# First pointwise stage of a convolution block: split weights, tap products on ScalarE, tap sums in PSUM

## The reference

```python
def conformer_conv(h, w_pw1, b_pw1, w_dw, b_dw, ln_g, ln_b, w_pw2, b_pw2):
    u = h @ w_pw1 + b_pw1                  # 2048 -> 4096: value and gate
    a, gate = jnp.split(u, 2, axis=-1)
    u = a * jax.nn.sigmoid(gate)
    u = depthwise_conv(u, w_dw, 31 taps, padding 15) + b_dw
    u = jax.nn.silu(layer_norm(u, ln_g, ln_b))
    return u @ w_pw2 + b_pw2
```

## Time and profile before

| | |
|---|---|
| time, median of 3 runs | 2646.93 us (2645.94 to 2649.62) |
| the profiled execution | 2647.79 us, of which its span of instructions 2645.9 us |
| PE busy | 2595.2 us, 98% of the span |
| DVE busy | 1874.5 us, 71% |
| ACT busy | 1232.9 us, 47% |
| POOL busy | 129.3 us, 5% |
| TensorE's mean granted clock | 0.99 of full speed |
| DMA | 560.60 MB, mean 212 GB/s |

### The profile page before, as it was taken

One profiled execution on the slowest core, in us unless ns is written; L12 is line 12 of the kernel. 1 busy time (PEld: TensorE's weight loads), 2 busy tenths in 40 slices (PEclk: granted clock), 3 DMA queues, 4 the chain that ended last, 5 costly groups with the idle time before them and its releaser, 6 DMA issues. The chain is left out here.

```text
span 2645.9 us, 40988 instructions
## 1 busy us (share of the span) xinstructions
PE 2595.2 (98%) x15425; PEld 2277.4 (86%) x15425; DVE 1874.5 (71%) x2655; ACT 1232.9 (47%) x1617; POOL 129.3 (5%) x203
## 2 busy tenths in 40 slices
PE   6999899999999999999999999999999999999998
PEld 4899898888888888888888888888888888888887
DVE  3468778887888888855666659999776644566554
ACT  3345544445645556544555541105554443444443
POOL 0021122001010000000000000000000000000000
PEclk8999999999999999999999999999999999999999
DMA  9998699768786877755666554554666655666554
GB/s 367 334 306 252 210 271 298 220 199 248 236 267 211 256 249 245 233 189 187 190 189 188 187 159 144 151 153 132 190 186 190 189 187 188 191 186 189 189 183 135
DMA packets 525076, 560.60 MB, mean 212 GB/s; under 512 B 20453, under 2 KB 487841, under 8 KB 524688
## 3 DMA queue, kind: packets, MB, share of 16 engines
q1 hardware_dynamic: 504448, 487.39, 58.1%
q0 software_dynamic: 20496, 71.38, 9.0%
...
...
## 5 line engine op out<-in xcount | busy, mean ns | idle before, releaser
L1126 DVE TENSOR_TENSOR wlo<-raw,whi 128x1024 fp32r<-128x1024 f32 x794 | 970.4, 1224 | 663.8 <-ACT whi L697 657.2
L697 ACT CAST whi<-raw 128x1024 fp32r<-128x1024 f32 x794 | 830.7, 1050 | 1037.1 <-PE ps L1944 896.5
L1942 PE MATMUL ps<-xhl,whi 128*128 128x512 f32 x3584 | 1130.6, 397 | 3.6 <-DVE xhl L1204 2.1
L1944 PEld LDWEIGHTS ps<-xhl,wlo 128*128 128x128 f32 x3584 | 674.3, 188 | 159.5
L1944 PE MATMUL ps<-xhl,wlo 128*128 128x256 f32 x3584 | 705.0, 278 | 0.0
L1942 PEld LDWEIGHTS ps<-xhl,whi 128*128 128x128 f32 x3584 | 547.0, 189 | 7.2 <-issue 5.1
L1942 PE MATMUL ps<-ghl,whi 128*128 128x512 f32 x1024 | 319.5, 393 | 0.0
L1944 PEld LDWEIGHTS ps<-ghl,wlo 128*128 128x128 f32 x1024 | 192.2, 188 | 44.5
L2304 PE MATMUL ps<-xg,raw 128*128 128x256 f32 x1024 | 221.5, 379 | 0.0
L1942 PE MATMUL ps<-fhl,whi 128*128 128x512 f32 x704 | 219.3, 392 | 0.0
L2304 PEld LDWEIGHTS ps<-xg,raw 128*128 128x128 f32 x1024 | 194.5, 190 | 26.4
...
## 6 DMA issues: line engine op xcount, KB each, us to landing
...
raw<-in_ffn_w_up SPq DMA_DIRECT2D x128, 512.0 KB, 3.7
raw<-in_ffn_w_down SPq DMA_DIRECT2D x128, 512.0 KB, 3.4
...
raw<-in_conv_w_pw SPq DMA_DIRECT2D x128, 256.0 KB, 3.2
```

The costliest lines, as they stand in the source:

```text
L697: nc.scalar.copy(whi[t % SPL][:, :, :], raw[t % RAW][:, :, :]).then_inc(s_hi, 1)
L1126: nc.vector.tensor_tensor(wlo[t % SPL][:, :, :], raw[t % RAW][:, :, :], whi[t % SPL][:, :, :].bitcast(F32), ALU.subtract).then_inc(s_lo, 1)
L1942: mm(o[:, m, :, :], whi[t % SPL][:, c, m * P:(m + 1) * P], x, start=first and c == 0, stop=last and c == KC - 1, skip_group_check=True)
L1944: ins = mm(o[:, m, 0, :], wlo[t % SPL][:, c, m * P:(m + 1) * P], x[:, 0, :], start=False, stop=last and c == KC - 1, skip_group_check=True)
```

## The change

Units of chunks 2 to 15 are split as everywhere else, with ACT making `whi` and POOL making `wlo` (`weights_low`, L757 of the changed kernel); PE makes the three products as six matmuls of 256 columns for each 128 inputs (`split_unit`). Chunks 0 and 1 stay full float32. DVE's four `gained_normed` go to a temporary, from which ACT makes the high halves and DVE and POOL two low quarters each (`quad_low`). A chunk's 31 taps are dealt out: ACT makes the products of taps 21 to 30 in five pairs (`pair`) and tap 1 alone, and begins the even sum (`sums_begun`); DVE adds taps 2 to 20 (and tap 0 from chunk 4 on) to two sums that now lie in PSUM (`tap_added`, L1826), adds four of the pairs to the first one (`pair_added`, L1833, 128x512 in SBUF), adds the PSUM sums (`sums_gathered`, L1847) and joins the halves (`chunk_added`, L1852). `glu` (L1877) of chunk c + 1 stands in the middle of chunk c's taps and reads the value from PSUM. `add_pair` and `add_square` move to POOL. PE's diagonal taps are now 8 for chunk 14 and 16 for chunk 15.

```diff
-TENSOR_TAPS = {14: range(27, TAPS), 15: range(14, TAPS)}
-GLU_15_AT = 20
-FIRST_SHIFTED = 3
+PAIRS = 5
+PAIRED = TAPS - 2 * PAIRS
+TENSOR_TAPS = {14: range(13, PAIRED), 15: range(5, PAIRED)}
+FIRST_SHIFTED = 4
...
+def vector_taps(c):
+    own = range(0 if c >= FIRST_SHIFTED else 2, min(TENSOR_TAPS.get(c, (PAIRED,))))
+    return [tap for tap in own if tap != 1]
...
+def value_gate_bank(c):
+    return ps[(G_PW1 + c) % 2][:, 0, :, :]
+def tap_sums(c):
+    return ps[c % 2][:, 1, :, :]
+def tensor_taps_bank(c):
+    return (bank_z, bank_f)[c % 2][:, 0:T]
+def gathered(c):
+    return products[:, c % 2, :, :]
...
+    def weights_low(t):
+        pool.wait_ge(s_hi, nth_split(t) + 1)
+        if t < T_PW1 + N_RAW + SPL:
+            pool.wait_ge(s_used, t + 1)
+        if t == T_PW1 + N_RAW:
+            pool.wait_ge(s_lo, RAW + nth_split(t))
+        nc.gpsimd.tensor_tensor(wlo[t % SPL][:, :, :], raw[t % RAW][:, :, :], whi[t % SPL][:, :, :].bitcast(F32), ALU.subtract).then_inc(s_lo, 1)
+    def add_pair(s):
+        pool.wait_ge(s_near, 1)
+        pool.wait_ge(s_dwd, 2 * s + 2)
+        if s > 1:
+            pool.wait_ge(s_pair, s - 1)
+        first = ucv[:, 0:2, :] if s == 1 else by_pairs[:, :, :]
+        nc.gpsimd.tensor_tensor(by_pairs[:, :, :], first, ucv[:, 2 * s:2 * s + 2, :], ALU.add).then_inc(s_pair, 1)
+    def add_square(p):
+        pool.wait_ge(s_csq, p + 1)
+        if p > 1:
+            pool.wait_ge(s_cold, p - 1)
+        nc.gpsimd.tensor_tensor(older, older, newest, ALU.add).then_inc(s_cold, 1)
+    weights_low(T_PW1 + 8)
+    weights_low(T_PW1 + 9)
+    quad_low(2)
+    weights_low(T_PW1 + 10)
+    quad_low(3)
+    for t in range(T_PW1 + 11, T_PW2):
+        weights_low(t)
+        s, at = divmod(t - T_PW1 - 21, 8)
+        if at == 0 and s > 0:
+            add_pair(s)
+        if at == 0 and s > 1:
+            add_square(s - 1)
+    add_square(5)
+    add_pair(6)
+    add_square(6)
...
+    def gate_sigmoid(c):
+        gate_c = value_gate[:, c % 2, 1, :]
+        gate_in = gate_c
+        if c < 2:
+            act.wait_ge(s_free[(G_PW1 + c) % 2], free_at(G_PW1 + c))
+        else:
+            gate_in = value_gate_bank(c)[:, 1, :]
+            glu_done(act, c - 2)
+            done(0, T_PW1 + 4 * (c + 1))
+        nc.scalar.activation(gate_c, gate_in, ACT.Sigmoid, bias=col("conv_b_pw1_2", DC + c)).then_inc(s_gsig, 1)
+    def tap_product(out, c, tap, bias=None):
+        src, w = upad[:, c, tap:tap + T], col("conv_w_dw_2", DC * tap + c)
+        if bias is None:
+            return nc.scalar.activation(out, src, ACT.Copy, scale=w)
...
+    def sums_begun(c):
+        even, odds = tap_sums(c)[:, 0, :], tap_sums(c)[:, 1, :]
+        bias = col("conv_b_dw_2", c)
+        glu_done(act, c)
+        act.wait_ge(s_edge, 2)
+        if c > 1:
+            act.wait_ge(s_dwd, c - 1)
+        if c < FIRST_SHIFTED:
+            tap_product(even, c, 0, bias).then_inc(s_bias, 1)
+        else:
+            act.wait_ge(s_piv, 1)
+            nc.scalar.activation(even, varr[:, :], ACT.Identity, scale=-1.0, bias=bias).then_inc(s_bias, 1)
+        tap_product(odds, c, 1).then_inc(s_bias, 1)
+    def pair(c, i):
+        if i == 0:
+            out = gathered(c)
+            if c == 0:
+                act.wait_ge(s_xnl, 4)
+            if c > 1:
+                act.wait_ge(s_padd, PAIRS * (c - 1))
+        else:
+            j = (PAIRS - 1) * c + i - 1
+            out = products[:, 2 + j % 2, :, :]
+            if j > 1:
+                before = divmod(j - 2, PAIRS - 1)
+                act.wait_ge(s_padd, PAIRS * before[0] + before[1] + 1)
+        for m in range(2):
+            ins = tap_product(out[:, m, :], c, PAIRED + 2 * i + m)
+        ins.then_inc(s_prod, 1)
...
+        gate_sigmoid(c)
+        sums_begun(c)
+        for i in range(PAIRS):
+            if 1 <= c < 15 and i < 4:
+                split_hi(0, T_PW1 + 4 * c + 8 + i)
+            pair(c, i)
+        if 2 <= c < 14:
+            diagonals(2 * (c - 2), 2)
         if c == 5:
             conv_square(0)
-            conv_square(1)
-        if c in (8, 10, 12, 14):
-            conv_square(c // 2 - 2)
-    for q in range(SPL):
-        split_hi(0, T_PW2 + q)
+        if c % 2 and c > 4:
+            conv_square((c - 3) // 2)
...
+    def tap_added(c, k):
+        own = vector_taps(c)
+        tap = own[k]
+        if k == 0:
+            dve.wait_ge(s_bias, 2 * c + 2)
+        if tap - 2 in own:
+            dve.wait_ge(s_tap, taps_before(c) + own.index(tap - 2) + 1)
+        sums = tap_sums(c)[:, tap % 2, :]
+        nc.vector.scalar_tensor_tensor(sums, upad[:, c, tap:tap + T], col("conv_w_dw_2", DC * tap + c), sums, ALU.mult, ALU.add).then_inc(s_tap, 1)
+    def pair_added(c, i):
+        dve.wait_ge(s_prod, PAIRS * c + i + 1)
+        if i > 1:
+            dve.wait_ge(s_padd, PAIRS * c + i - 1)
+        nc.vector.tensor_tensor(gathered(c), gathered(c), products[:, 2 + ((PAIRS - 1) * c + i - 1) % 2, :, :], ALU.add).then_inc(s_padd, 1)
+    def tensor_taps_added(c):
+        dve.wait_ge(s_dwt, c - 13)
+        dve.wait_ge(s_padd, PAIRS * (c + 1) - 1)
+        sv.did(nc.vector.tensor_tensor(gathered(c)[:, 0, :], gathered(c)[:, 0, :], tensor_taps_bank(c), ALU.add))
+    def sums_gathered(c):
+        dve.wait_ge(s_tap, taps_before(c + 1))
+        dve.wait_ge(s_padd, PAIRS * (c + 1) - 1)
+        if c in TENSOR_TAPS:
+            sv.wait()
+        nc.vector.tensor_tensor(gathered(c), gathered(c), tap_sums(c), ALU.add).then_inc(s_padd, 1)
+    def chunk_added(c):
+        dve.wait_ge(s_padd, PAIRS * (c + 1))
+        nc.vector.tensor_tensor(ucv[:, c, :], gathered(c)[:, 0, :], gathered(c)[:, 1, :], ALU.add).then_inc(s_dwd, 1)
...
-            dve.wait_ge(s_free[(G_PW1 + c) % 2], free_at(G_PW1 + c))
-            nc.vector.tensor_tensor(upad[:, c, PAD:PAD + T], value, gate_c, ALU.mult).then_inc(s_u, 1)
...
+        gate_c = value_gate[:, c % 2, 1, :]
...
+        value, made = (value_gate[:, c, 0, :], s_u) if c < 2 else (value_gate_bank(c)[:, 0, :], s_free[(G_PW1 + c) % 2])
+        nc.vector.scalar_tensor_tensor(upad[:, c, PAD:PAD + T], value, col("conv_b_pw1_2", c), gate_c, ALU.add, ALU.mult).then_inc(made, 1)
...
+    for c in range(15):
+        for k in range(len(vector_taps(c))):
+            tap_added(c, k)
+            if k == 1 and c:
+                sums_gathered(c - 1)
+            if k == 3 and c:
+                chunk_added(c - 1)
+            if k == 5 and c == FIRST_SHIFTED:
+                first_less_pivot()
+            if k == 6 and c == FIRST_SHIFTED - 1:
+                pivot()
+            if k == 7 and c == 0:
+                rooted(1)
+            if k == (10 if c else 12):
+                glu(c + 1)
+            if c < 14 and k in (6, 9, 12, 15):
+                pair_added(c, k // 3 - 1)
+            if c == 14 and k in (4, 6, 8, 9):
+                pair_added(c, (4, 6, 8, 9).index(k) + 1)
+    tap_added(15, 0)
+    tensor_taps_added(14)
+    tap_added(15, 1)
+    tap_added(15, 2)
+    sums_gathered(14)
+    tap_added(15, 3)
+    pair_added(15, 1)
+    chunk_added(14)
+    for i in range(2, PAIRS):
+        pair_added(15, i)
+    tensor_taps_added(15)
+    sums_gathered(15)
+    chunk_added(15)
...
+    def split_unit(t, c, q):
+        pe.wait_ge(s_lo, RAW + nth_split(t) + 1)
+        if c == 2:
+            pe.wait_ge(s_xnl, q + 1)
+        for i in range(KC):
+            k = KC * q + i
+            for w, half in ((whi, 0), (whi, 1), (wlo, 0)):
+                for m in range(PC):
+                    ins = mm(value_gate_bank(c)[:, m, :], w[t % SPL][:, i, m * P:(m + 1) * P], xhl[:, k, half, :],
+                             start=k == 0 and w is whi and half == m == 0, stop=k == DC - 1, skip_group_check=True)
+        ins.then_inc(s_used, 1)
...
+    def shared_taps(c):
+        first = 0 if c == 14 else len(TENSOR_TAPS[14])
+        glu_done(pe, c)
+        pe.wait_ge(s_edge, 2)
+        pe.wait_ge(s_diag, first + len(TENSOR_TAPS[c]))
+        for i, tap in enumerate(TENSOR_TAPS[c]):
+            ins = mm(tensor_taps_bank(c), diag[:, first + i, :], upad[:, c, tap:tap + T], start=i == 0, stop=tap == PAIRED - 1)
+        ins.then_inc(s_dwt, 1)
...
-            full(T_PW1 + 4 * c + q, G, q, c == 0, xg if c < 2 else xn)
+            t = T_PW1 + 4 * c + q
+            if c < 2:
+                full(t, c, q, c == 0)
+            else:
+                split_unit(t, c, q)
```

More of the change, by code:

```diff
@@ L73 @@
 N_PW1 = 16 * 4
+N_RAW = 2 * 4
 T_PW2 = T_PW1 + N_PW1
@@ L953, in _, with normed_high @@
             root(3)
[L956 to L965 removed]
+            def normed_high(q):
+                act.wait_ge(s_xn, q + 1)
+                nc.scalar.copy(xh[:, 4 * q:4 * q + 4, :], xtmp[:, q % 2, :, :]).then_inc(s_xnh, 1)
@@ L967, in conv_square, with diagonals @@
+            tensor_taps = [(c, tap) for c, taps in TENSOR_TAPS.items() for tap in taps]
+            def diagonals(first, n):
```

(4 more changed lines are left out.)

243 lines of the change are left out of this document (94 added, 149 removed).

## The result

The changed kernel takes 2704.48 us (median of 4 runs, 2702.97 to 2705.9) against 2647.05 us (4 runs, 2645.94 to 2649.62): 1.0214 times as long, 95% interval 1.0201 to 1.0226. The forecast was 2705.

The account below looks back on a forecast made before the run. PE and DVE were both taken as full before; after, DVE's gate waits and turns with POOL set the pace. 2647.8 - 0.7 + 53 (chunk turns) + 6 (start turns) = 2706 us, given as 2705; 8-in-10 range 2634 to 2722.

Parts of the forecast that it names:

- PE's chunk, 11.4 us: PE's six split matmuls per block, 16 blocks of 0.71 us, take 11.4 us a chunk against 13.8 before.
- DVE's own work, 11.8 us: DVE's taps, additions and gate multiplication of a chunk from 4 on, without long waits, take 11.8 us.
- a tap of 0.40 in PSUM: Each DVE tap summing into PSUM starts 0.40 us behind the last, with bounds 0.34 and 0.48.
- The dearer PSUM access: DVE's access time of 125 ns on PSUM against 60 on SBUF might add 1.3 us a chunk, 17 us in all.
- The wait at the gate: Before each next chunk's glu, DVE idles for ACT's sigmoid, 1.7 us in even and 2.2 in odd chunks.
- POOL's subtraction, 2.52 us: Each 1024-column weights_low on POOL takes 2.52 us, upper bound 2.69.
- Turns: DVE additions with two SBUF operands and POOL instructions alternate whole, costing 4.1 us a chunk, 53 us; 2705 us, chance 0.50.
- The ends: Stage start and end: without turns it ends 0.7 us earlier than before; turns at the start add 6 us.
- the second: Rival: DVE and POOL run side by side, each of five additions taking twice its time, 36 us; 2683 us, chance 0.17.
- The third: Rival: DVE and POOL don't disturb each other, only the gate's wait stands; 2647 us, no difference, chance 0.18.
- the zero price: Lower bound for POOL beside DVE: two-SBUF-operand additions lose nothing to POOL's instructions.
- The fourth: Rival: PSUM taps are cheap, 0.38 us or less, without turns; 2631 us, bounded by POOL near 2624, chance 0.15.

Follow-up runs that it names:

- experiment 6: Changed kernel with the pair sums of chunks 0 to 13 in a spare PSUM tile and the next chunk's sigmoid issued ahead of the last pair; 2631.55 us.
- experiment 4: Changed kernel with POOL clearing the low halves of chunks 2 to 15 by memset, reading nothing, where it subtracted; 2647.86 us.
- experiment 5: Changed kernel with the pair sums of chunks 0 to 13 in a spare PSUM tile, so additions read SBUF once; POOL's subtractions kept; 2655.76 us.
- run 14: Not a follow-up run: in "chunk 14 run 14 us before", "run" is a verb, said of the diagonals of chunk 14.
- experiments 1: Changed kernel with DVE adding the product pairs into the taps' own PSUM tile, so each addition has one operand in PSUM; 2675.68 us.
- (8): Changed kernel with POOL copying raw to wlo, reading one SBUF operand, where it subtracted; 2661.34 us in one run.
- experiment 9: Changed kernel with the taps' sums in SBUF instead of PSUM, giving every tap two SBUF operands; 2779.87 us in one run.
- experiment 3: Changed kernel with the pairs added into the taps' PSUM tile and the sigmoid issued ahead of the fifth pair; 2652.95 us.

## Why the prediction was right

Point by point, in its own order.

- **PE's chunk, 11.4 us.** Right: 11.52 in experiment 6. As foretold, it counted for nothing while others took longer. In the changed kernel PE is busy 75% of the steady part and not two thirds, since at a granted clock of 0.87 the same matmuls take longer.
- **DVE's own work, 11.8 us, and a tap of 0.40 in PSUM.** Right: experiment 6 runs at 11.74, and the taps have 479 ns on average and start 0.40 apart. The dearer PSUM access that the prediction weighed is not seen.
- **The wait at the gate, 1.7 and 2.2 us.** The idle time is 1.52 and 2.04, but it begins at the end of a tap, 0.48 behind its start, where I had counted 0.40; from the start of `pair_added` to `glu` it is 2.60 us in chunk 8 where I had 2.7, so in my terms the wait is 1.6. The sigmoid is 0.45 long for my 0.51. Turn-free periods are 13.31 and 13.93 (experiment 4) against 13.5 and 14.0.
- **POOL's subtraction, 2.52 us.** Too dear: 2.35 at least, and a median of 2.41 where hardly anything collides (experiment 5); its mean is 2.60 with DVE's additions between.
- **Turns.** Right in mechanism and size, not in form. Between `glu(1)` and `glu(14)` they cost (1845.05 - 1618.89) - (1788.71 - 1614.00) = 51.5 us, where I had 53. By chunk it was 3.4 (even) and 18.42 - 13.93 = 4.5 (odd), where I had 4.7 and 3.5. In the even chunk the same three instructions are blocked as in my count, each for less. POOL's fourth subtraction ends 12.5 us behind `glu`, not 13.7, mostly because each of the four is shorter than my 2.52. The rest is that a turn of DVE's puts POOL back by 0.5 or 0.2 us (2.84 and 2.58 against 2.35), where I had 0.7 and 0.4. In the odd chunk 7 four instructions are blocked, by 1.7, 0.9, 1.0 and 1.0 us; my 3.5 does not say which it counted. That the mean came out at 3.95 for my 4.1 is luck: one error is 1.3 us down, the other 1.0 up. "0.1 us behind the end of a POOL instruction, with idle time before them" was wrong too: the blocked instruction starts on time in the records and its *duration* grows. One who looked only for idle time would have found none and called DVE busy.
- **The ends.** Turns at the start: 1618.89 - 1614.00 = 4.9 us for my 6. The turn-free stage was to end 0.7 us before the old end and ended with the memsets 0.1 us behind it. Two errors cancel in this: `glu(14)` comes at 1788.71, not 1792.5, and the end behind it is 4.6 us longer. Of these 3 are the 16 diagonals: they take 10.00 us there and 10.17 in the changed kernel for 32 rows, 0.32 each, where I took 0.22 from the earlier trace rows. The granted clock is 0.70 while they run in the changed kernel, so partly PE's lower level, and 1.00 while the 8 diagonals of chunk 14 run 14 us before, at 3.72 for 16 rows, 0.23 each. In between PE stood idle for 5.0 us without a break. I had named this effect, at up to 7 us, and kept it out of the sum; it was 3.
- **The sum** by durations, each group's excess over the same instructions alone: L1833 82.7 - 64 x 0.69 = 38.5; L1852 19.4 - 16 x 0.42 = 12.7; L1884, the low quarters and one more instruction of 1024 columns 5.5. 56.7 us in all, and the difference to experiment 4 is 56.6. The forecast of 2705 lies 0.5 us from the median, but its terms were off by 1 to 2 us each (51.5 for 53, 4.9 for 6, 0.1 behind the old end for 0.7 before it): the mechanism and the size were foretold, the last microsecond was not.

The rivals: the second (each slowed to twice its time) falls with the distribution 675/693/2543 and with the ends 0.55 us behind POOL's. The third is what the change would be without turns, and experiment 4 is that kernel. (Where the prediction calls the zero price "the second case", it means this third one.) The fourth needed a tap below 0.38 and none of the turns. That two SBUF operands on DVE and one on POOL are the condition is shown from both sides: by taking DVE's away (experiments 1, 5), POOL's away (4), leaving POOL one (8), and giving DVE more (9). The Trainium skill (SBUF — State Buffer, Who interferes with whom) says that a DVE instruction with two SBUF inputs and a GpSimd instruction that reads SBUF shut each other out for a whole instruction. With that the trace agrees, with 2.38 us for an addition of 0.68.

Left open: where the odd chunk's four turns depart from my count, how the turns of experiment 9 fall, and 0.1 to 0.4 us a chunk in experiment 3.
